# Later convolution rows normalized early and parked in activation slots, the gate's norm on VectorE, weights in halves, loads in a written order

## The reference

```python
def conformer_conv(a, gate, conv_w, conv_b, ln_g, ln_b):
    u = a * jax.nn.sigmoid(gate)
    u = lax.conv_general_dilated(u, conv_w..., feature_group_count=D_A) + conv_b   # 31 taps, 512 channels
    return jax.nn.silu(layernorm(u, ln_g, ln_b))
def even_mixer(h, ...):                      # layer 0
    z = h @ w_in                             # 1024 -> a, gate, p of 512 each
    ya = conformer_conv(a, gate, conv_w, conv_b, ln_g, ln_b)
    yb = multiscale_pool(p, pool_w, pool_scale)
    return jnp.concatenate([ya, yb], axis=-1) @ w_out
def spatial_gating(u, v, v_ln_g, v_ln_b, spatial_w, spatial_b):
    vn = layernorm(v.reshape(bn, s, N_SGU, H_D), v_ln_g, v_ln_b)      # 4 heads of 128
    sv = jnp.einsum('hqk,bnkhc->bnqhc', spatial_w, vn_in_chunks_of_128) + spatial_b
    return u * sv
def odd_mixer(h, ...):                       # layer 1: c, u, v of 512 each; u, v behind a gelu
    return jnp.concatenate([fourier_mix(c, fourier_w), spatial_gating(u, v, ...)], axis=-1) @ w_out
def swiglu(h, w_gate, w_up, w_down):         # 1024 -> 2816 -> 1024
    return (jax.nn.silu(h @ w_gate) * (h @ w_up)) @ w_down
```

## Time and profile before

| what | us |
|---|---|
| median of 3 runs | 2695.94 (2694.18 to 2806.41) |
| the profiled execution | 2678.49 |
| its span on the slowest core, core 6 | 2676.4 |
| spans of the other seven cores | 2657.3 to 2661.6 |
| TensorE busy in the span | 2545.3 |

### The profile page before, as it was taken

One profiled execution on the slowest core, in us unless ns is written; L12 is line 12 of the kernel. 1 busy time (PEld: TensorE's weight loads), 2 busy tenths in 40 slices (PEclk: granted clock), 3 DMA queues, 4 the chain that ended last, 5 costly groups with the idle time before them and its releaser, 6 DMA issues.

```text
span 2676.4 us, 38177 instructions; the slowest of 8 cores (2657.3 to 2676.4 us)
## 1 busy us (share of the span) xinstructions
PE 2545.3 (95%) x12585; PEld 1193.9 (45%) x12739; DVE 802.3 (30%) x1166; ACT 665.8 (25%) x1186; POOL 385.2 (14%) x655
## 2 busy tenths in 40 slices
PE   5899799889999999999999979999999999999998
PEld 2346444334444444444444446444444444444443
DVE  2334543312222222221212456232222222222212
ACT  2433534301211111111125664111111112111111
POOL 1110122201110111011001441221011101100100
PEclk7999999999999999999999989999999999999999
DMA  6796689945665698355462227996366546644522
GB/s 151 183 192 135 134 147 177 169 132 122 126 120 151 124 158 152 130 97 83 116 167 103 32 61 163 168 165 124 114 123 127 112 116 124 126 122 97 78 48 95
DMA packets 336618, 338.46 MB, mean 126 GB/s; under 512 B 166560, under 2 KB 294448, under 8 KB 336304
## 3 DMA queue, kind: packets, MB, share of 16 engines
q0 software_dynamic: 120016, 118.40, 30.9%
q1 hardware_dynamic: 206768, 208.71, 29.3%
q10 hardware_dynamic: 9648, 8.92, 1.1%
HBM read 331.92 MB, written 83.89 MB: 155 GB/s over the span
## 4 chain that ended last, share of the span: by engine, by line
PE 86%; DMA 3%; SPq 3%; issue 2%; POOL 2%; DVE 2%; ACT 2%; another core or an unknown queue 1%; ACTq 0%; DVEq 0%; POOLq 0%
PE ps L171 86%; SPq L185 2%; DMA xin_51<-x 2%; ACT vt_12615 L1114 1%; DMA xr_3357<-x 1%; DVE hb_98 L393 1%; POOL vn_12617 L1118 0%; DMA wd_3891<-ffn_wd 0%; POOL rs_12620 L1091 0%; DMA wd_16768<-ffn_wd 0%; ACT hb_98 L387 0%; DMA gbc_62<-norm_g 0%; POOL ssb_44 L373 0%; DVE bst_2112 L825 0%
## 5 line engine op out<-in xcount | busy, mean ns | idle before, releaser
L171 PE MATMUL ps<-BIG_43,wgu_3356 128*128 128x512 bf16 x2816 | 616.6, 381 | 7.0 <-DVE xr_3357 L484 6.6
L171 PE MATMUL ps<-BIG_43,wgu_16418 128*128 128x512 bf16 x2816 | 612.4, 379 | 0.0
L171 PEld LDWEIGHTS ps<-BIG_43,wgu_3356 128*128 128x128 bf16 x2816 | 275.7, 98 | 343.1 <-issue 13.5
L171 PEld LDWEIGHTS ps<-BIG_43,wgu_16418 128*128 128x128 bf16 x2816 | 275.2, 98 | 332.6
L171 PE MATMUL ps<-wd_3891,gT_3892 128*128 128x512 bf16 x1376 | 305.3, 382 | 10.1 <-DMA wd_3891<-ffn_wd 8.4
L171 PE MATMUL ps<-wd_16768,gT_16769 128*128 128x512 bf16 x1376 | 305.3, 382 | 6.5 <-DMA wd_16768<-ffn_wd 4.8
L510 DVE TENSOR_TENSOR gT_16769<-tmp_16770,ps 128x512 bf16<-128x512 f32 x176 | 120.9, 687 | 425.7 <-PE ps L171 425.7
L510 DVE TENSOR_TENSOR gT_3892<-tmp_3893,ps 128x512 bf16<-128x512 f32 x176 | 120.9, 687 | 417.6 <-PE ps L171 367.3
L171 PEld LDWEIGHTS ps<-wd_3891,gT_3892 128*128 128x128 bf16 x1408 | 138.2, 98 | 177.2 <-issue 12.6
L171 PEld LDWEIGHTS ps<-wd_16768,gT_16769 128*128 128x128 bf16 x1408 | 138.2, 98 | 173.5 <-issue 9.0
L508 ACT ACTIVATE tmp_16770<-ps 128x512 f32<-128x512 f32 x176 | 104.5, 594 | 402.4 <-PE ps L171 392.9
(11 more groups left out here) (160 smaller groups left out, 1715.6 us busy)
## 6 DMA issues: line engine op xcount, KB each, us to landing
wgu_3356<-ffn_wgu POOLq DMA_DIRECT2D x88, 512.0 KB, 6.6
wgu_16418<-ffn_wgu POOLq DMA_DIRECT2D x88, 512.0 KB, 6.3
xr_3357<-xres SPq DMA_DIRECT2D x32, 512.0 KB, 4.1
xnat<-xr_3357 SPq DMA_DIRECT2D x32, 512.0 KB, 3.2
xr_16419<-xr SPq DMA_DIRECT2D x32, 512.0 KB, 4.0
out<-xr_16419 SPq DMA_DIRECT2D x31, 512.0 KB, 2.9
xin_51<-x SPq DMA_DIRECT2D x28, 512.0 KB, 5.1
xr_3357<-x SPq DMA_DIRECT2D x28, 512.0 KB, 5.5
```

Of the source, the lines that this page charges most:

```text
L171: ins = self.nc.tensor.matmul(o, lhsT=l, rhs=r, start=st, stop=sp)
```

## The change

- **First projection.** A tile of zeros serves for a dummy Sigmoid at the start and a dummy Silu ahead of the prologue. The weights are loaded in the order p whole, then the first halves (256 columns) of gate and a, then the second halves; `ag_half` computes tiles 0 to 3 in halves. x2 to x5 wait for the p block, later tiles for the first half of a. `norm_step` loads two tiles ahead, then transposes, scales and squares, one tile later each; the projection of p runs two tiles ahead of `ag`; there are five hb slots. `tr_pe` always evacuates on DVE.
- **LayerNorm.** Groups are pairs up to tile 15, then fours. Tiles below 16 are transposed on TensorE. The normalized rows of tile t from 16 on are written into BIG's slot t + 1 (the last to vn31) during the up phase; `bgd0` issues their transposes in the down phase of chunk 0, three per i, and their Silu from i = 5.
- **First prologue.** Groups 0 to 3 are prepared ahead or early, with eight banks; the norm vector stays in SBUF and is copied to PSUM behind it.
- **Gate.** One root per tile, subtract and multiply on DVE, no negation; `sv` comes four tiles behind the projection.
- **Layer 1's `ffn`.** w_down blocks 10 to 17 are loaded during the Fourier stage; xp lies at 72 KB and is loaded one step later.

```diff
-                evac(t % 2, BIG[:, t, :, :], pv, [psd[b], psd[b + 1]], dB[t])
+                evac(1, BIG[:, t, :, :], pv, [psd[b], psd[b + 1]], dB[t])
...
-                    if c == 0:
+                    if c == 0 and j not in have:
                         dma_runs(pool, wd[:, j, :], T["ffn_wd"][l, j], writes=[d_wd[j]])
...
                     if 1 <= i < 8:
                         s_load(i)
+                    if bgd is not None:
+                        bgd(c, i)
...
+        for i, hs in ((WP, (0, 1)), (WG, (0,)), (WA, (0,)), (WG, (1,)), (WA, (1,))):
...
+        k.op(act, lambda e: e.activation(out=silw[:, 0:2], in_=silw[:, 0:2], func=AF.Sigmoid), writes=[d_silw])
...
-            k.dma(sp, [(x, T["x"][t])], writes=[d])
+            k.dma(sp, [(x, T["x"][t])], reads=[] if t < 2 else d_w[WP] if t < 6 else [d_w[WA][0]], writes=[d])
...
+        def ag_half(t, h):
+            bl = []
+            for w in (WG, WA):
+                b = k.banks(1)
+                bl.append(b)
+                k.mm([(ps[:, b, 0:256], BIG[:, t, kk, :], w_in[:, w, kk, 256 * h:256 * h + 256], kk == 0, kk == 7)
+                      for kk in range(8)], reads=[d_w[w][h]] + dB[t], writes=[psd[b]])
...
-        jobs = [(p_proj, t) for t in range(8)]
-        for t in range(NT):
+        jobs = [(p_proj, t) for t in range(6)] + [(lambda t: ag_half(t, 0), t) for t in range(4)]
+        jobs += [(lambda t: ag_half(t, 1), t) for t in range(4)]
+        for t in range(4, NT):
+            if t + 2 < NT:
+                jobs.append((p_proj, t + 2))
             jobs.append((ag, t))
-            if t + 8 < NT:
-                jobs.append((p_proj, t + 8))
...
-            if 2 <= i - 2 < NT:
-                n_tr(i - 2)
-            if 2 <= i - 1 < NT:
-                n_stat(i - 1)
+            if 8 <= i + 2 < NT:
+                n_load(i + 2)
+            if 0 <= i - 3 < NT:
+                n_tr(i - 3)
+            if 0 <= i - 1 < NT:
                 nrm.scale(i - 1)
-            if 8 <= i < NT:
-                n_load(i)
+            if i < NT:
+                n_stat(i)
...
-            while ni[0] < min(t + (4 if t < 6 else 6) if fn == p_proj else t + 14, NT + 2):
-                norm_step()
+            if fn == p_proj:
+                while ni[0] < min(t + 5 if t < 6 else t + 8, NT + 3):
+                    norm_step()
...
-        groups = [(0, 2), (2, 4), (4, 6), (6, 8), (8, 10), (10, 13), (13, 16), (16, 20), (20, 24), (24, 28), (28, 32)]
+        groups = [(2 * i, 2 * i + 2) for i in range(8)] + [(16, 20), (20, 24), (24, 28), (28, 32)]
...
-                if n >= LN_PE:
-                    k.dma(sp, [(BIG[:, t, 0:4, :], v)], reads=[d_v], writes=[dB[t][0]], transpose=True)
...
+        def vn_at(t):
+
+            return (BIG[:, t + 1, 0:4, :].rearrange("p c q -> p (c q)"), dB[t + 1][0]) if t < NT - 1 else vn31
+
+        def vn_tr(t):
+            v, d_v = vn_at(t)
+            k.dma(sp, [(BIG[:, t, 0:4, :], v)], reads=[d_v], writes=[dB[t][0]], transpose=True)
...
-        LN_PE = 5
+        LN_PE = 8
...
+        k.nb = 8
+        k.op(act, lambda e: e.activation(out=silw[:, 0:2], in_=silw[:, 0:2], func=AF.Silu), writes=[d_silw])
         prologue(op, 2, 2, feed0)
+        k.nb = 6
+        gps = ps[:, 6:8, :].rearrange("p b n -> p (b n)")
+        k.op(dve, lambda e: e.tensor_copy(out=gps, in_=gbc1[0]), reads=gbc1[1], writes=[psd[6], psd[7]])
...
+            for n in range(4):
+                if j == n:
+                    ln_stat(4 + n)
+                    ln_norm(4 + n)
+                if j == n + 1:
+                    ln_silu(4 + n)
+                if j == 2 * n + 4:
+                    ln_stat(8 + n)
+                if j == 2 * n + 5:
+                    ln_norm(8 + n)
...
+        def bgd0(c, i):
+            if c == 0:
+                for t in range(16 + 3 * (i - 1), min(19 + 3 * (i - 1), NT)):
+                    if t >= 16:
+                        vn_tr(t)
+                if i >= 5 and i % 2 == 1 and i < 9:
+                    ln_silu(8 + (i - 5) // 2)
+                if i >= 9:
+                    ln_silu(8 + i - 7)
...
-                k.op(act, lambda e: e.activation(out=vt[:, t % 8, h * 128:(h + 1) * 128],
-                                                 in_=vt[:, t % 8, h * 128:(h + 1) * 128], func=AF.Identity,
-                                                 scale=rs[:, r, 0, ti, h:h + 1], bias=rs[:, r, 1, ti, h:h + 1]),
-                     reads=[d_vt[t % 8], d_rs4[r][ti]], writes=[d_vt[t % 8]])
+                k.op(dve, lambda e: e.tensor_scalar(out=vt[:, t % 8, h * 128:(h + 1) * 128],
+                                                    in0=vt[:, t % 8, h * 128:(h + 1) * 128],
+                                                    scalar1=mv[:, r, ti, h, 0:1], scalar2=rs[:, r, 0, ti, h:h + 1],
+                                                    op0=ALU.subtract, op1=ALU.mult),
+                     reads=[d_vt[t % 8], d_mv[r], d_rs4[r][ti]], writes=[d_vt[t % 8]])
...
-            if i >= 8:
-                sv(i - 8)
+            if i >= 4:
+                sv(i - 4)
...
-            if i >= 6:
-                v_norm(i - 6)
+            if i >= 2:
+                v_norm(i - 2)
...
+        for n in range(2):
+            sv(NT - 4 + n)
+            f_gcs_part(0, 8 * n)
+            f_gcs_part(0, 8 * n + 4)
+            if n == 0:
+                v_norm(NT - 1)
...
+                wdt = k.lazy("wd", 108 * KB, [D], BF16, NJ)
+                for j in range(10, 18):
+                    dma_runs(pool, wdt[0][:, j, :], T["ffn_wd"][1, j], writes=[wdt[1][j]])
+            if h == 2:
+                xpt, d_xpt = k.buf("xp", 72 * KB, [D], F32, 4)
```

More of the change, by code:

```diff
@@ L746, in p_load @@
                       reads=[d_pdr[t // 16], d_pdr[(t + n - 1) // 16]], writes=d_[t - lo:t - lo + n])
-        jobs = [(p_proj, t) for t in range(8)]
-        for t in range(NT):
+        jobs = [(p_proj, t) for t in range(6)] + [(lambda t: ag_half(t, 0), t) for t in range(4)]
[3 more added lines that the diff above has]
+                jobs.append((p_proj, t + 2))
             jobs.append((ag, t))
-            if t + 8 < NT:
-                jobs.append((p_proj, t + 8))
         gscale0()
-        for t in range(2):
-            n_stat(t)
-            nrm.scale(t)
-            n_tr(t)
-        ni = [2]
+        ni = [0]
         def norm_step():
@@ L840, in ln_norm @@
             for t in range(t0, t1):
-                v, d_v = vn.next()
+                if t < 16:
+                    v, d_v = vn.next()
+                else:
+                    v, d_v = vn_at(t)
                 k.op(act, lambda e: e.activation(out=v, in_=z[t // 16][:, t % 16, :], func=AF.Identity,
@@ L935, in prologue @@
                 feed(i)
-            op.nrm.hb = hbr
             op.xr = xr
@@ L1084, in v_stat @@
                      reads=[d_bst[ti]], addw=[d_mv[r]])
-        def v_rs(tg):
-            r = tg % 2
-            k.op(pool, lambda e: e.tensor_tensor(out=rs[:, r, 0], in0=mv[:, r, :, :, 1],
-                                                 in1=cst_[:, 1, 0:16].rearrange("p (a b) -> p a b", a=4), op=ALU.add),
-                 reads=[d_mv[r], d_cst_], writes=d_rs4[r])
-            k.op(pool, lambda e: e.tensor_tensor(out=rs[:, r, 0], in0=rs[:, r, 0],
-                                                 in1=cst_[:, 0, 0:16].rearrange("p (a b) -> p a b", a=4), op=ALU.pow),
-                 reads=d_rs4[r] + [d_cst_], writes=d_rs4[r])
         def v_rs1(t):
@@ L1237, in build @@
             f_s1(1, range(8 * n, 8 * n + 8, 4))
-        for n in range(4):
-            sv(NT - 4 + n)
+        for n in range(2):
+            sv(NT - 2 + n)
         wo, d_wo = load_w_out("od_w_out", 168 * KB)
         gbc3, gscale3 = load_gbc(3, 202 * KB, True)
-        xpt, d_xpt = k.buf("xp", 128 * KB, [D], F32, 4)
-        for i in range(4):
-            k.dma(sp, [(xpt[:, i], xnat[i])], reads=[d_xnat[0]], writes=[d_xpt[i]])
         f_mix(1)
@@ L1255, in build @@
                 gscale3()
+                wdt = k.lazy("wd", 108 * KB, [D], BF16, NJ)
[3 more added lines that the diff above has]
+                xpt, d_xpt = k.buf("xp", 72 * KB, [D], F32, 4)
+                for i in range(4):
+                    k.dma(sp, [(xpt[:, i], xnat[i])], reads=[d_xnat[0]], writes=[d_xpt[i]])
         Wf = Weights(1, 152 * KB)
@@ L1278, in bg1 @@
                 gsf()
-        ffn(1, Wf, op, None, gfin, xr, xr1, d_xr1, bg1)
+        ffn(1, Wf, op, None, gfin, xr, xr1, d_xr1, bg1, wdt=wdt, have=range(10, 18))
         k.barrier()
```

112 lines of the change are left out of this document (55 added, 57 removed).

## The result

The changed kernel took 2647.8 us against 2695.3 us for the kernel before, ratio 0.9822 with a 95% interval of 0.980 to 0.9845. That lies inside the range of 2602 to 2668, 19 us above the forecast of 2629. In a second series of five rounds it took 2644.9 against 2675.1 us, ratio 0.9893 (0.9869 to 0.9916). Executions of the kernel before in which a pair of cores had a granted clock of 0.97 instead of 0.98 took 2692 to 2698 us in the later series, the others mostly 2665 to 2678; the clocks of the first series' executions are not on record, but by their 2694 to 2696 us they stand with the former. The second series has no such pair, so the change itself is worth some 30 us. That agrees with the profiled executions, 2678.49 and 2645.65 us. Against the profile my sum of 67 us is twice too large, and the base of 2696 hid a part of that.

What follows compares the result with a forecast made beforehand. TensorE, busy 95% of the span, was the bound, so gains come from its gaps and slow-clock time. Terms 26 + 13 - 5 + 11 + 0 + 20 + 2 = 67 us off 2678.49 give 2611.5, or 2629 beside the median; range 2602 to 2668.

Steps and rivals of the forecast that it cites:

- First projection, +26: Start to 232 us: ordered loads and fewer row waits end the stage at 205; 26 us gained, bounds 10 and 36.
- First output projection, +13: Layer 0, 294 to 348 us: earlier table load, groups prepared ahead, eight banks; 13 us gained, bounds 5 and 17.
- Up phase, -5: Layer 0, 350 to 500 us: 24 more TensorE transposes and waits for ACT's norm; 5 us lost, bounds -9 and -1.
- The 22 transposes, +11: DMA transposes leaving layer 0's up phase end the lag at 500 to 560 us; 11 us gained, bounds 2 and 15.
- Parked rows, 0: Down phase of chunk 0: 16 transposes chained on SP fit within the phase; 0 us, bounds -15 and 0.
- rival (c): Chunk 0's down phase: parked rows transpose at 15.1 us each; up to 165 us slower, 2794 us; chance 4%.
- The gate norm, +20: 1460 to 1600 us: norm moved from ACT to DVE, one POW per tile; 20 us gained, bounds 6 and 27.
- I take 252: Gate loop: each of a tile's four subtract-multiplies on DVE was assumed to take 252 ns, not 491.
- below 4.7: Gate loop: the new chain takes 3.8 us a tile, less than TensorE's own 4.7 us of work.
- Rival (b): Gate stage no faster: four operations of 491 ns each; that part yields 4 us, total 2645 us; chance 12%.
- Layer 1's loads, +2: Layer 1: w_down blocks 10 to 17 early, xp at other bytes; 2 us gained, bounds -2 and 5.
- rival (d): Timed runs' slowest core owes its 17 us to the crowded up phase, so this goes too; 2605 us; chance 9%.

Runs made afterwards that it cites:

- E7: The kernel before with the ordered loads of the first stage alone; 2643.8 to 2652.7 us, convolution starting at 205.7 to 207.8 us.
- E10: E9 without layer 1's early w_down loads, its x tiles at the old place, x tiles 2 and 3 not waiting for p weights; 2622.7 us, ratio 0.9818.
- E5: The changed kernel with a sixth x slot and the loads of tiles 6 and 7 three tiles later in layer 0's first output projection; fastest execution 2642.3 us.
- E6: The changed kernel with two of the four first up-weight fetches moved to the end of layer 0's first output projection; 2643.6 us.
- E9: The changed kernel with E2, E3, E5 (loads two tiles later), and two up-weight fetches at the start, the rest at i = 6; 2622.4 us, ratio 0.9817.
- E8: The changed kernel with the parking alone undone: rows 16 to 31 go through vn and are transposed at once; 2647.9 to 2648.3 us.
- E3: The changed kernel with the four norm instructions of a gate tile not waiting for one another; gate stage 256.2 to 258.2 us, fastest execution 2632.4 us.
- E2: The changed kernel with one more tile of lag in the gate loop; gate stage 256.8 to 258.1 us, fastest execution 2631.1 us.
- E4: The changed kernel with a tile's statistics and POW issued ahead of the previous tile's norm and multiply; gate stage 266.5 to 272.4 us, fastest execution 2641.0 us.

## Why the prediction held, and where its sum did not

- **First projection, +26: 25.8 us on core 6, 21 to 27 on the others.** The size is right, shown by E7, and the stage ends at 207 instead of 205. My steps were partly wrong: the first matmul comes at 18.1, not 15, because the p block took 15.4 us from issue to landing, and the longest wait is for tile 2 (7.61 us). Tile 6, which I had as the late one at some 10 us, costs 2.34, and by another way: ACT's square waits 3.75 us for its load, and the evacuation into pst that TensorE needs before tile 5's transposes stands behind it. E7 and E10 show that these arrivals can shift by 3 to 10 us without moving the end.
- **First output projection, +13: 6.0 on core 6, 7.7 to 12.5 on the others.** The chain of LayerNorm and tables went as I said. What I left out is the other end: I counted the stage as over when its matmuls are, but the first `up` needs four DMA transposes, which stand on SyncE behind loads that wait for stores. The matmuls end 37.8 us after the stage's start, sooner than my 41.5; the 9.85 us of wait behind them are this term's miss. E5 takes that wait on the transposes away and gains only 3.2 us, so SyncE's order is a part of the cause and the load on the DMA queues (E6) another.
- **Up phase, -5: -5.5 to -7.3 on seven cores.** Right, with waits for ACT's norm of 3.7 us. But E6 and E9 show that it and the stage ahead are one account: what the first gains, 6.4 and 7.9 us on the mean, the second mostly gives back, 6.0 and 5.5.
- **The 22 transposes, +11: about +9 on core 6**, whose up phase shortens by 3.6 us against the others' 6 us of loss. E8 shows that parking spares single cores up to 8 us through ACT's wait for vn buffers; and as other cores are then the slowest, only 0 to 3 us of it reach the time. On core 6 before it was the late x tile, as I had it: ACT's waits for vn buffers there are 9.8 us, but TensorE waits only 0.2 us for ACT, and 6.6 us for the add of an x tile whose load stands on SyncE behind the transposes:

```profile
483.59 17.02 SPq L185 DMA_TRANSPOSE BIG_43<-vn_3355  x4
...
507.09 0.53 SPq L185 DMA_DIRECT2D xr_3357<-x  x1
```

- **Parked rows, 0: 0.** They land in 2.4 to 6.8 us, the first in 13.6, and chunk 0's down phase takes 83.2 to 85.9 us, 82.2 to 83.6 before (core 6 87.2); rival (c) is refuted.
- **The gate norm, +20: -3.9 on core 6, -2.9 to -8.3 on the others. This is the step that failed**, at "I take 252" and "below 4.7". The form of the chain was right, its size was not: the norms take 1.71 us, not 1.0, because each waits for the one before through the buffer that they share, and hand-offs are larger; 4.66 us instead of 3.8. And 4.7 us for TensorE was a mean over four tiles, of which one carries the u projection. In the other three TensorE has less work than the chain (E9, where the chain no longer holds it, takes 2.9 us for most of them), and two tiles of lag are too few to even that out. My own sign of being wrong, "the per-tile loop ends last", came true. Rival (b) had this result for a reason that is near it (dear norms), with a yield of 4. E3 and E2 each give 14 us back, E9 some 23: then the stage is 16 to 19 us shorter than before, close to the +20 that I had counted.
- **Layer 1's loads, +2: 0** by E10. The rule of the Trainium skill on the port pair (page "SBUF — State Buffer", section "SBUF: two separate sides") decided nothing: in the timeline after, the norms never meet POOL's multiply. On core 3 of E2, E4 and E9 four norms start in the last 0.36 to 0.44 us of a multiply; each ends 0.08 to 0.09 us behind it and lasts 0.44 to 0.52 us instead of 0.345. That would fit the rule, at a cost of 0.1 to 0.2 us each.

On core 6 the measured terms are 25.8 - 1.1 (convolution, which I had not counted) + 6.0 + 3.6 + 5.4 (rest of layer 0) - 3.9 - 4.9 (layer 1's output projection and up phase) = 31 us, against 32.0 between the spans. The first up matmul comes 30.8 us sooner than before, not 40. That the time beside the median came so near the forecast is luck: the 17 us between median and profile went away, as in rival (d), but not for its reason, and, as far as the times tell, because of the clock of single pairs of cores. Without them the same parts would have given some 2665 us, still inside the range, but at its edge. (The 2605 of rival (d) is a slip: 2629 - 17 is 2612.)

## What to carry to other kernels

Add up a loop's chain by iteration, with its semaphores, and compare it with the shortest iteration of the engine that it feeds, not with the mean. Where it is longer than the shortest, a tile more of lag is a cheap thing to try (14 us in E2) before anything is moved between engines. A stage ends when the next one can start: follow every queue to the last transfer that the next stage's first instruction needs. Before a sum is set beside a median, ask for the clock of the cores in the executions that made it.

## What the runs showed of the hardware

- Four DVE operations of 128x128 f32 with two pointers take 1.11 us back to back and 1.71 us with a semaphore between each two; one lasts 344 to 350 ns on average in both. The cost of an operation and the distance between two are different numbers.
- The POW on POOL takes 1.01 us for 4 columns; that is about as long as the four norms when these are free of one another.
- Bytes moved sooner for one stream delayed the other: with two x tiles (1 MB) ahead of it, the p block's first use came at 20.8 to 22.7 us in E10 instead of 17.5 to 19.3 in E9, while tile 2's transposes came 7 us sooner on core 3 (24.2 instead of 31.1).
